# VectorE's difference of a weight unit placed one unit of eight tiles sooner in its order

## The chip, the cores and the metric

The kernel runs on one core of a Trainium2 chip. What counts is the device time of one execution in microseconds (us), the median of the runs; lower is better. A core has TensorE (PE, matrix products), VectorE (DVE), ScalarE (ACT), GpSimd (POOL) and SyncE (SP), which issues the loads. Each engine works through its own list of instructions in order, and waits at an instruction until the semaphores that it names have been raised.

## The reference

Two transformer blocks are computed in float32, one behind the other, for 256 tokens of width 2048, and the final norm:

- Block one: `mod = silu(c) @ w_ada`, six vectors that shift, scale and gate; `h = rmsnorm(x) * (1 + scale) + shift`; `p = h @ w_in`; a latent attention branch (norm, `w_uq`, `w_ukv`, rotary, causal softmax, `w_o_mla`); a gated delta rule branch (causal convolution of width 4 and silu on 24 groups of 128 channels, unit length rows, a triangular solve in chunks of 64, a running state, `w_o_gdn`); both gated by sigmoids and joined by `w_o`; then `silu(gate) * up` through `w_gate_up` and `w_down`.
- Block two: norm, `w_in_2`; a convolution of width 31 with layer norm and silu on half the channels and a neighbourhood attention with 16 heads on the other half; `w_out_2`; then `relu(h @ w_up_2) ** 2 @ w_down_2`, and the last norm.

## The kernel before, in words

All the weight matrices are cut into tiles of 128 x 128, put into one stream in the order in which PE uses them (6848 tiles), eight to a **unit** of 128 x 1024 floats, 512 KB. To keep accuracy in PE's float32r format, a unit is split in two: **HI**, the rounded weights (ACT, function hi, L566: a copy into float32r), and **LO**, what the rounding left (VectorE, function lo, L722: raw minus HI). The activations are split in the same way (split_hi on ACT, split_lo on VectorE, L758 and L760), and PE adds three products for a tile: in pairs of tiles L360, L361, L363 and L364 (called wide), else L366 to L368; for the last matrix L375 to L377, four tiles a step (tile_tokens). So PE can't begin a unit until its LO is there.

Buffers: RAW has 5 slots for loaded units, HI and LO have 3 each (NHL). HI and LO of unit v therefore overwrite those of unit v - 3, and wait until PE has ended that unit. RAW's slot is free when LO has run. Among the units of the stream stand others ("A" in the list of kinds), 512 KB each, of w_ada; these go through no PE, VectorE multiplies and sums each in one instruction (unit_dot, L710).

The order is written by one walk through the program (walk). Every engine goes through the same walk and puts down only its own instructions, so the place of a call in the walk is its place in the order of its engine. Products are made by blocks (16 tiles make one output of 128 columns, for a matrix with 2048 rows), and each block, when it ends, leaves a generator with its evacuation and what follows from it (later). Such generators, of attention and the delta rule too, stand in a list, and flush takes a step of each that is due: after tiles 1, 3, 5 and 7 of a unit, with at least LAG = 3 tiles from a step to the next, EVLAG = 4 before the first.

The feeding of units is also in that walk. At the end of unit u (i == 7) blocks sets unit_pe[u], calls feed(u + AHEAD), and then flush. feed(n) puts down the HI of all units up to n that have none (hi_part), then goes through the slots up to unit n in order (proc_next: lo for a unit of the stream, unit_dot for one of w_ada, and behind each the loads that it makes room for, load_next), and last it looks one unit on: if unit n + 1 has no HI yet, its load is put down and PE's end of the unit whose buffer it takes is known, its HI is put down as well. tile_tokens does the same from the function tokens. With AHEAD = 2 the end of unit u thus puts down LO(u+2) and, behind it, HI(u+3).

Names used below. g_less (L912) subtracts a product from MT or UU in the delta rule, and g_turn_mt (L467) transposes the outcome on PE; g_level (L908) and g_rows (L916) are neighbours of it on VectorE, g_copy (L671) on ACT, g_pair (L473) on PE. taps (L816) are three instructions of the convolution of width 4, followed by tanh (L581) and the next tap_first (L648) on ACT. rope_turn is L421. copy_sum (L570) and sum_halves (L726) evacuate a bank. SP's loads of the stream are L334.

Of the kernel before, what the change touches and what calls it, by code (L numbers as in the profile page):

```python
# [4 lines left out]

T = 256
NRAW, NEARLY, NHL = 5, 8, 3
LAG, EVLAG, AHEAD = 3, 4, 2
N_TILES = 6848
N_ADA = 192  # L10
LATE = [(2, 0), (2, 1), (3, 1), (4, 1), (3, 0), (4, 0), (5, 0), (5, 1)]
# [2556 lines left out]
```

## Time and profile before

| | before |
|---|---|
| median of 3 runs | 2768.66 us |
| lowest, highest | 2768.32, 2770.45 us |
| profiled execution, its own time | 2770.82 us |
| its span, first to last instruction | 2768.3 us |
| mean granted clock of PE in it | 0.992 of 2.4 GHz |
| PE busy | 2693.1 us, 97% |
| VectorE busy | 1932.0 us, 70% |
| ACT busy | 1318.2 us, 48% |
| POOL busy | 152.4 us, 6% |
| DMA, mean | 204 GB/s |

In the profile's rows L12 is line 12 of the kernel. A name such as LO<-RAW,HI gives what an instruction writes and reads. A matmul's end is modelled, since matmuls overlap in PE. "Idle before" is the engine's idle time in front of an instruction, with what ended it behind the arrow.

### The profile page before, as it was taken

To read this page: it belongs to the slowest core of one execution; us is meant where nothing else is said; L and a number is where in the kernel's file an instruction comes from. 1 tells how busy PE (TensorE), PEld (TensorE's weight loads), DVE (VectorE), ACT (ScalarE), POOL (GpSimd) and SP (SyncE) were. 2 spreads that over 40 slices of the span, in tenths; PEclk is the share of its full clock that TensorE was granted. 3 is DMA by queue.
4 is the path that set the end of the run, shared out by engine and by line. 5 is a ranking of instruction groups with operands and counts; after the bars stand their busy time and mean duration, and the time that the engine had idled before them with its cause. 6 is when DMAs were issued, how large, how long until landed. Compare 5 with 4: busy or idle time off the path is not lost.

```text
span 2768.3 us, 41005 instructions
## 1 busy us (share of the span) xinstructions
PE 2693.1 (97%) x16144; PEld 2386.3 (86%) x16144; DVE 1932.0 (70%) x2982; ACT 1318.2 (48%) x2063; POOL 152.4 (6%) x132
## 2 busy tenths in 40 slices
PE   8989999999999999999999999999999999999998
PEld 7778978888899888888888889998888888888887
DVE  6777778866886886566555678997667466575665
ACT  2175644433544544444444454467564444443443
POOL 0000000000002000000000170211100000000000
PEclk9999999999999999999999999999999999999999
DMA  9944358656796786555555555554545555655554
GB/s 387 409 142 157 106 183 276 225 191 198 266 317 215 256 297 208 191 189 190 187 188 191 187 177 165 184 166 138 170 154 177 195 190 191 194 186 197 189 191 145
DMA packets 158737, 565.17 MB, mean 204 GB/s; under 512 B 17617, under 2 KB 21841, under 8 KB 158417
## 3 DMA queue, kind: packets, MB, share of 16 engines
q1 hardware_dynamic: 158544, 562.56, 59.9%
q8 instruction: 127, 2.08, 0.3%
q14 instruction: 66, 0.53, 0.1%
HBM read 560.39 MB, written 2.10 MB: 203 GB/s over the span
## 4 chain that ended last, share of the span: by engine, by line
PE 86%; DVE 6%; ACT 3%; DMA 3%; issue 1%; DVEq 0%; POOL 0%; ACTq 0%; SPq 0%
PE BK L363 17%; PE BK L361 17%; PE BK L364 8%; PE BK L360 8%; PE BK L366 5%; PE BK L368 5%; PE BK L367 5%; PE BK L377 4%; PE BK L376 4%; PE BK L375 4%; PE BK L473 2%; DVE LO L722 2%; DMA EARLY<-wada_dram 1%; ACT HI L566 1%; PE BK L388 1%
## 5 line engine op out<-in xcount | busy, mean ns | idle before, releaser
L566 ACT ACTIVATE HI<-RAW 128x1024 fp32r<-128x1024 f32 x824 | 874.9, 1062 | 1182.0 <-PE BK L361 636.7
L722 DVE TENSOR_TENSOR LO<-RAW,HI 128x1024 fp32r<-128x1024 f32 x824 | 1012.3, 1229 | 384.8 <-ACT HI L566 383.6
L363 PE MATMUL BK<-H,HI 128*128 128x512 f32 x2160 | 871.6, 406 | 18.9 <-DVE LO L722 18.2
L361 PE MATMUL BK<-H,HI 128*128 128x512 f32 x2128 | 842.0, 397 | 0.0
L364 PE MATMUL BK<-H,LO 128*128 128x256 f32 x2160 | 602.6, 279 | 0.0
L360 PE MATMUL BK<-H,LO 128*128 128x256 f32 x2128 | 596.5, 280 | 0.2 <-DVE H L760 0.2
L360 PEld LDWEIGHTS BK<-H,LO 128*128 128x128 f32 x2128 | 402.0, 189 | 94.0 <-DVE H L760 0.6
L364 PEld LDWEIGHTS BK<-H,LO 128*128 128x128 f32 x2160 | 409.3, 189 | 84.9 <-issue 1.0
L363 PEld LDWEIGHTS BK<-H,HI 128*128 128x128 f32 x2160 | 412.5, 191 | 32.6 <-DVE LO L722 23.1
L361 PEld LDWEIGHTS BK<-H,HI 128*128 128x128 f32 x2128 | 401.7, 189 | 3.8
L366 PE MATMUL BK<-H,HI 128*128 128x256 f32 x1280 | 377.4, 295 | 7.1 <-DVE LO L722 6.4
L368 PE MATMUL BK<-H,LO 128*128 128x256 f32 x1280 | 363.9, 284 | 0.0
L367 PE MATMUL BK<-H,HI 128*128 128x256 f32 x1280 | 363.7, 284 | 0.0
L366 PEld LDWEIGHTS BK<-H,HI 128*128 128x128 f32 x1280 | 246.8, 193 | 10.7 <-DVE LO L722 8.2
L367 PEld LDWEIGHTS BK<-H,HI 128*128 128x128 f32 x1280 | 246.9, 193 | 1.4
L368 PEld LDWEIGHTS BK<-H,LO 128*128 128x128 f32 x1280 | 246.5, 193 | 0.0
L375 PE MATMUL BK<-HI,H 128*128 128x512 f32 x512 | 199.2, 389 | 0.0
L377 PE MATMUL BK<-HI,H 128*128 128x512 f32 x512 | 199.2, 389 | 0.0
L376 PE MATMUL BK<-LO,H 128*128 128x512 f32 x512 | 199.2, 389 | 0.0
L760 DVE TENSOR_TENSOR H<-TV,H 128x256 fp32r<-128x256 f32 x116 | 49.1, 425 | 171.5 <-ACT H L577 171.5
L376 PEld LDWEIGHTS BK<-LO,H 128*128 128x128 f32 x512 | 96.1, 188 | 20.1
L375 PEld LDWEIGHTS BK<-HI,H 128*128 128x128 f32 x512 | 96.1, 188 | 19.9
(266 smaller groups left out, 2555.0 us busy)
## 6 DMA issues: line engine op xcount, KB each, us to landing
RAW<-wst_dram SPq DMA_DIRECT2D x837, 512.0 KB, 3.4
RAW<-wada_dram SPq DMA_DIRECT2D x155, 512.0 KB, 4.6
EARLY<-wada_dram SPq DMA_DIRECT2D x37, 512.0 KB, 11.0
EARLY<-wst_dram SPq DMA_DIRECT2D x19, 512.0 KB, 12.2
X<-xT_dram SPq DMA_DIRECT2D x8, 512.0 KB, 7.0
B<-bias_dram SPq DMA_DIRECT2D x32, 128.0 KB, 3.4
out_dram<-B SPq DMA_DIRECT2D x8, 256.0 KB, 2.2
B<-gain_dram SPq DMA_DIRECT2D x1, 1024.0 KB, 4.8
```

The costliest lines, as they stand in the source:

```text
L360: e.matmul(bk[:, 256:512], ll, H[:, k, 0:256], start=False, stop=False, skip_group_check=True)
L361: e.matmul(bk[:, :], hh, H[:, k, :], start=False, stop=last, skip_group_check=True).then_inc(S["tile"], 1)
L363: e.matmul(bk[:, :], hh, H[:, k, :], start=first, stop=False, skip_group_check=True)
L364: e.matmul(bk[:, 256:512], ll, H[:, k, 0:256], start=False, stop=last, skip_group_check=True).then_inc(S["tile"], 1)
L366: e.matmul(bk[:, 0:256], hh, H[:, k, 0:256], start=first, stop=False, skip_group_check=True)
L367: e.matmul(bk[:, 0:256], hh, H[:, k, 256:512], start=False, stop=False, skip_group_check=True)
L368: e.matmul(bk[:, 0:256], ll, H[:, k, 0:256], start=False, stop=last, skip_group_check=True).then_inc(S["tile"], 1)
L375: e.matmul(bks[m][:, :], H[:, k, 128 * m:128 * m + 128], hh, start=first, stop=False, skip_group_check=True)
L376: e.matmul(bks[m][:, :], H[:, k, 128 * m:128 * m + 128], ll, start=False, stop=False, skip_group_check=True)
L377: r = e.matmul(bks[m][:, :], H[:, k, 256 + 128 * m:384 + 128 * m], hh, start=False, stop=last, skip_group_check=True)
L566: e.activation(HI[:, u % NHL, :], raw_at(slot), ACT.Copy).then_inc(S["hi"], 1)
L722: e.tensor_tensor(LO[:, u % NHL, :], raw_at(slot), HI[:, u % NHL, :].bitcast(f32), sub).then_inc(S["lo"], 1)
```

## The change

AHEAD goes from 2 to 3, so the end of unit u calls feed(u + 3). That puts down HI(u+3) and then the slots up to unit u+3, LO(u+3) the last of them. The look one unit on finds that PE's end of unit u + 1 isn't known yet and puts down nothing. HI(u+3) has the place that it had; LO(u+3), the unit_dots of the slots between LO(u+2) and LO(u+3), and the loads behind them, stand one unit sooner. The start (feed(w.tile // 8 + 2), after the direct products) is as it was.

```diff
--- before.py
+++ after.py
@@ -5,7 +5,7 @@
 
 T = 256
 NRAW, NEARLY, NHL = 5, 8, 3
-LAG, EVLAG, AHEAD = 3, 4, 2
+LAG, EVLAG, AHEAD = 3, 4, 3
 N_TILES = 6848
 N_ADA = 192
 LATE = [(2, 0), (2, 1), (3, 1), (4, 1), (3, 0), (4, 0), (5, 0), (5, 1)]
```

## Rows read from the trace of the kernel before

**Rows 1.** Page, part 1: busy us (share of the span) xinstructions.

```profile
PE 2693.1 (97%) x16144; PEld 2386.3 (86%) x16144; DVE 1932.0 (70%) x2982; ACT 1318.2 (48%) x2063; POOL 152.4 (6%) x132
```

**Rows 2.** Waits of PE, VectorE and SP: us in total, times, longest us.

```profile
PE BK L363 <- DVE LO L722: 18.2, 12, 5.3
...
PE BK L366 <- DVE LO L722: 6.4, 4, 4.3
...
DVE LO L722 <- ACT HI L566: 383.6, 357, 4.5
...
SPq L334 <- DVE LO L722: 1866.3, 765, 14.3
```

**Rows 3.** Timeline, quiet stage (start us, us, instruction [idle before]); busy us by engine 1040-1590.

```profile
1100.47 1.06 ACT L566 ACTIVATE HI<-RAW 128x1024 fp32r<-128x1024 f32 x1 [1.45 <-PE BK L361]
1101.57 1.23 DVE L722 TENSOR_TENSOR LO<-RAW,HI 128x1024 fp32r<-128x1024 f32 x1 [0.57 <-ACT HI L566]
...
1103.26 1.06 ACT L566 ACTIVATE HI<-RAW 128x1024 fp32r<-128x1024 f32 x1 [1.72 <-PE BK L364]
...
1040.00:1590.00 550.00, 549.76 (x3154) 479.30 (x3153) 330.54 (x440) 259.90 (x371) 9.57 (x8) 1.00 0.57 191
```

**Rows 4.** Timeline of PE: two waits for LO and one for ACT.

```profile
166.46 0.80 PE L363 MATMUL BK<-H,HI 128*128 128x512 f32 x1 [5.33 <-DVE LO L722]
...
321.05 0.33 PE L499 MATMUL BK<-CN,B 128*128 128x128 f32 x1 [1.49 <-ACT B L644]
...
509.00 0.50 PE L363 MATMUL BK<-H,HI 128*128 128x512 f32 x1 [2.07 <-DVE LO L722]
```

**Rows 5.** Stretches: length, PE, PEld, DVE, ACT, POOL busy, granted clock, DMA share, GB/s.

```profile
165.79:172.62 6.83, 6.16 (x20) 5.30 (x21) 4.51 (x11) 6.72 (x9) 0.00 (x0) 0.50 0.29 93
...
510.54:513.95 3.41, 3.41 (x14) 3.03 (x13) 3.34 (x8) 3.38 (x5) 0.00 (x0) 0.50 0.97 381
...
321.05:324.46 3.41, 3.41 (x30) 3.41 (x31) 1.68 (x5) 2.80 (x8) 0.00 (x0) 1.00 0.49 157
```

**Rows 6.** Timeline of one level of the delta rule; all instructions of L912.

```profile
628.37 1.06 ACT L566 ACTIVATE HI<-RAW 128x1024 fp32r<-128x1024 f32 x1 [2.47 <-PE BK L368]
...
628.00 0.68 DVE L912 TENSOR_TENSOR X<-X,BK 128x512 f32<-128x512 f32 x1
...
629.52 0.60 PE L467 MATMUL BK<-CN,X 128*128 128x128 f32 x4
...
L912 DVE TENSOR_TENSOR X<-X,BK x20: 677/687/690, 283.7 to 662.2; 128x512 f32<-128x512 f32 x20
L912 DVE TENSOR_TENSOR B<-B,BK x8: 679/686/693, 359.9 to 684.1; 64x512 f32<-64x512 f32 x8
```

**Rows 7.** Instructions of L816, 176 to 222; timeline of ACT behind one group.

```profile
L816 DVE SCALAR_TENSOR_TENSOR TV<-B,CO,TV x30: 475/482/485, 179.5 to 219.5; 128x255 f32<-128x255 f32 x10, 128x254 f32<-128x254 f32 x10, 128x253 f32<-128x253 f32 x10
...
193.62 1.52 DVE L816 SCALAR_TENSOR_TENSOR TV<-B,CO,TV 128x255 f32<-128x255 f32 x3
...
195.18 0.42 ACT L581 ACTIVATE B<-TV 128x256 f32<-128x256 f32 x1 [1.56 <-DVE TV L816]
...
196.16 1.05 ACT L566 ACTIVATE HI<-RAW 128x1024 fp32r<-128x1024 f32 x1
```

**Rows 8.** Timeline of ACT, VectorE and PE in the mixed stage.

```profile
294.68 1.06 ACT L566 ACTIVATE HI<-RAW 128x1024 fp32r<-128x1024 f32 x1 [1.00 <-PE BK L368]
...
293.97 1.28 DVE L916 TENSOR_TENSOR X<-BK,B 128x512 f32<-128x512 f32 x2
...
296.18 0.59 PE L421 MATMUL BK<-B,CN 128*128 128x256 f32 x2
```

**Rows 9.** Timeline at a seam of the feed-forward part.

```profile
1077.44 0.42 DVE L726 TENSOR_TENSOR TV<-BK,TE 128x256 f32<-128x256 f32 x1
...
1077.98 1.06 ACT L566 ACTIVATE HI<-RAW 128x1024 fp32r<-128x1024 f32 x1 [1.46 <-PE BK L361]
...
1079.86 0.50 PE L363 MATMUL BK<-H,HI 128*128 128x512 f32 x1
```

## The prediction

> **What bounds the kernel now.** I read the page first, for the busy time by engine [rows 1]: TensorE (PE) is busy for 97% of 2768.3 us and VectorE (DVE) for 70%. So the time is PE's, and only PE's gaps can be gained or added. The view of waits by engine comes next [rows 2]. PE waited 18.2 + 6.4 = 24.6 us for VectorE's LO, in 16 waits; VectorE itself sat idle for 383.6 us, in 357 gaps, in front of LO until ACT's HI was there. The second number matters more: VectorE works in order and stops at an instruction whose signal is missing.
>
> The timeline of a quiet stage shows the clockwork [rows 3]. HI of unit v overwrites the buffer of unit v-3, so it starts when PE ends that unit: one HI every 2.79 us, 1.06 us long. LO follows 0.04 us behind HI, 1.23 us long, although its place in the order is a unit later: VectorE has run ahead of PE to that place. PE is busy for 549.76 of the 550 us there. So LO can't come sooner in the quiet stages: HI isn't moved, and LO needs it.
>
> **What the change does.** feed(u + 3) at the end of unit u puts LO(u+3) where LO(u+2) stood. HI(u+3) was already put there by the look-ahead at the end of feed, so ACT's and PE's orders stay. With LO move the dots (L710) of the slots before it, and SP's loads, which follow each LO or dot. Nothing is added or removed; no load is larger.
>
> SP costs nothing: it waited 1866.3 us for LO in all [rows 2], so its queue has room, and a load can only be issued sooner. If a load did become late, HI would be, but it has the rest of two units, over 3 us.
>
> **Gain.** LO is no longer behind other VectorE work, so the 16 waits [rows 2] can go, 24.6 us. At six of them, the 5.33 us at 166.46 and the 2.07 us at 509.00 among them [rows 4], PE's granted clock then falls to 0.50, which is 1.2 GHz: for 6.83 us in two of the six cases (as at 165.79) and for 3.4 us in four (as at 510.54) [rows 5], 27.3 us, of which half, 13.7 us, is lost work. The ends are 0 and 38.3 us. I take 31: two of the waits lie in the stage of rows 7, where LO is late again.
>
> **Cost.** VectorE now stands at LO(u+3) until PE has ended unit u and HI is through, and only then does what stands behind: the steps put down at that unit's end. Those with a reader on PE four tiles later are late. One is seen whole [rows 6]. HI starts at 628.37, ends at 629.43; LO would then run from 629.5 to 630.7, and g_less (L912, now at 628.00, 0.68 us) end at 631.3 or 631.4. PE's transposes of it (L467) started at 629.52. So PE waits **1.9 us**. Before, LO's place there was filled by one whose HI had been ready for a unit.
>
> A. This repeats in the levels of the delta rule. L912 runs 20 + 8 times [rows 6]; going through the timeline I count 18 with a PE reader so close: 18 x 1.9 = **34 us**.
>
> B. In the mixed stage from 205 to 340 (convolution, latent attention and delta rule at once) the same happens to g_rows (L916 at 293.97, twice, 1.28 us): HI starts at 294.68, so the LO would end at 297.0 and L916 at 298.3 at the earliest, and PE's L421, which waits for its signal, ran at 296.18 [rows 8]: 2.1 us. I count ten such; taken at 1.8 us each, between A's size and this one's less what a few tenths of spare take off, they make 18 us.
>
> C. From 176 to 222 there is a loop through both engines: HI 1.05, LO 1.22, three taps 1.52, then from tanh at 195.18 to the next HI at 196.16 another 0.98 us [rows 7], 4.8 us with the hand-overs. Before, the taps stood behind the LO of the unit before, so a turn of the loop took in two units; now it is one, against PE's 2.8 us. x30 are ten units with taps [rows 7], 2.0 us each; LO's lead of some 3 us and the six units without taps give back 6: 14 us.
>
> D. Three seams of the feed-forward part (1080, 1331, 1571): L726 at 1077.44 begins the split whose end the tile at 1079.86 needs [rows 9]. Behind HI (from 1077.98) and LO it would begin at 1080.3, 2.9 us later. ACT's part of the split stands behind that HI today, which I estimate to give back 0.6 us: 2.2 us each, 6.7 in all.
>
> E. Three more at 2046 to 2058, where normed rows go VectorE, ACT, PE, by A's size: 6.
>
> F. Single ones (770 to 805, 1672, 1779, 1892): about 8, which no row fixes; ends 0 and 15.
>
> B to F are 53 us. Some fall into one unit, where one wait covers the other, so I take two thirds: **35 us**. Ends: 15 and 53. For A: half, 17, if VectorE often reaches the place late anyway, and 34.
>
> G. The clock again. A wait of 1.49 us at 321.05 cost no clock, and one of 2.07 did [rows 4, 5]. The new ones, near 1.9, lie between, nearer to the second. The 18 of A and some 12 of the others, by 1.7 us (half of 3.4), would be 51; the other end is 0. Since their sizes spread over the gap between the two rows, I take half, **25 us**.
>
> Sum: 34 + 35 + 25 - 31 = +63 us. The profiled execution took 2770.8 us (its span is 2768.3) and lies 2.2 us over the median of the runs, 2768.66. So 2770.8 + 63 - 2.2 = **2832 us**, 2.3% slower.
>
> The Trainium skill, Perfetto Trace Analysis, section Optimization Strategy, speaks for the change: find the gaps on the most contended engine, see what signal ends them, and make that dependency start sooner. The trace has such gaps, 24.6 us for LO; by that rule alone the sum would be the gain, -38 us, and the time that of R1 or a little less. The same page of the Trainium skill, section Sequencer Loop, has an engine's instruction wait in its queue until its semaphore is ready; the trace agrees, with 383.6 us of VectorE standing in front of LO.
>
> **Rivals.** R1, **faster**: VectorE has 30% of its time free and absorbs the standing; only the gain is left. It decides at the readers: if L912's result were due later than 631.4, A would be nothing. For it: 16 waits and six clock falls are real. Against: 629.52 is a reader's start on an engine that never idles. It gives 2768.7 - 31 = 2737 us. Chance 0.10.
>
> R2, **no difference**: LO already runs right behind HI in fact, so the new place changes nothing where it matters, or gain and cost cancel: A at half and B to F at their low end, 32, less 31. 2769 us. It also stands for the change not doing what it says. For it: rows 3. Chance 0.06.
>
> R3, **the loop of C in more stages**, with VectorE to ACT to HI in each unit, as in latent attention's tail and the convolution, and the clock falling at all new waits: 34 + 53 + 51 - 31 = 107, to 2876 us. For it: ACT feeds on VectorE in many stages, and VectorE is busy for 70% of the span [rows 1] even with nothing to stand for. Against: the loop bites only where it is longer than PE's unit in most units, and only x30 of L816, of all the taps, stand so close [rows 7]. Chance 0.20.
>
> **How the numbers follow.** The forecast has 0.64. Its own range takes A whole, B to F from 15 to 53 and G from 10 to 40, about 2797 to 2865. The range of 8 in 10 is 2778 to 2885: it leaves out R1, R2 and a tail of R3. A measurement of this kernel can tell about 0.2%, 5.5 us, from no change. Slower by more: 0.64 + 0.20 = 0.84; within it 0.06; faster 0.10.
>
> **What would show it.** Right: in the profile after, PE's waits for LO are near 0, but L467 and L473 wait for VectorE's X (L912), about 1.9 us each and over ten times; VectorE's idle time in front of LO grows beyond 383.6 us; the granted clock falls more often than before between 400 and 700; the stretches 1100 to 1300 and 2145 to 2700 take as long as before. Wrong: L467 with no wait for VectorE (A fails and R1 holds), or waits in every unit from 176 to 222 and at 1600 (R3). If A's waits are there with the clock at 1.00 throughout, G was too large, and the time is near 2807.

## The result, and the profile after

| | before | after |
|---|---|---|
| median | 2769.16 us (4 runs) | 2947.10 us (4 runs) |
| lowest, highest | 2768.32, 2770.45 us | 2940.32, 2953.70 us |
| span of the profiled execution | 2768.3 us | 2949.8 us |
| mean granted clock | 0.992 | 0.976 |

The changed kernel is slower by the factor 1.0643, interval 1.0617 to 1.0668: +178 us where +63 was forecast, outside the range of 2778 to 2885. The sign was right, the size was not.

The page of the changed kernel, part 1, answers to [rows 1], and its part 5 has LO:

```profile
PE 2748.5 (93%) x16144; PEld 2419.5 (82%) x16144; DVE 1930.4 (65%) x2982; ACT 1316.4 (45%) x2063; POOL 126.8 (4%) x132
...
L722 DVE TENSOR_TENSOR LO<-RAW,HI 128x1024 fp32r<-128x1024 f32 x824 | 1012.9, 1229 | 920.6 <-ACT HI L566 858.9
```

VectorE does the same work as before, 1930.4 us in 2982 instructions. What grew is its standing in front of LO: 858.9 us for HI, against 383.6 [rows 2]. PE's side has two parts. It is idle for 2949.8 - 2748.5 = 201.3 us, before 75.2: +126.1. And the same 16144 matmuls take 55.4 us longer, 2748.5 against 2693.1, at a lower clock. The two make the 181.5 us of the span. Most of the second part is the clock: the mean granted clock lacks 0.8% of 2768.3 us before, 22 us, and 2.4% of 2949.8 us after, 71 us. The difference of 49 us is an estimate from the two rows of the table.

The waits of the changed kernel, of PE, VectorE and SP's queue (us in total, times, longest):

```profile
PE BK L363 <- DVE LO L722: 28.4, 18, 5.6
PE BK L499 <- ACT B L644: 28.1, 18, 6.0
PE BK L467 <- DVE X L912: 17.2, 11, 2.8
...
PE BK L485 <- DVE B L912: 5.1, 3, 1.8
...
PE BK L473 <- DVE X L912: 3.3, 2, 1.7
...
DVE LO L722 <- ACT HI L566: 858.9, 642, 7.6
DVE LO L722 <- PE BK L361: 49.4, 34, 2.1
...
SPq L334 <- DVE LO L722: 2103.8, 765, 12.7
```

Two things are to be seen. The waits for LO, which the change should have ended, are there as before: 28.4 us for L363 alone, against 24.6 in all [rows 2]. They have moved: 19.0 us of them, in nine waits, lie in units 35 to 53 (8.5 us in two before), and none lies in units 103 to 184 (3.8 us in three before). And two families are new: readers of L912, 25.6 us in 16 waits, and L499 behind ACT's L644, 28.1 us in 18, of which 19.3 us in 12 lie in units 530 to 560. Over all rows of this view, PE's waits for VectorE went from 32.4 us in 24 to 116.5 in 78, and those for ACT from 26.3 us in 46 to 68.4 in 69.

Next, where it happened. I count time from the first matmul of one unit of the stream to that of another. The same stretches of work, before, as windows (length, PE, PEld, DVE, ACT, POOL busy, granted clock, DMA share, GB/s): units 35 to 53 (taps), 53 to 83 (mixed), 103 to 184 (delta rule), 530 to 560 (wide convolution and neighbourhood attention):

```profile
158.20:224.60 66.40, 57.51 (x299) 49.03 (x298) 54.43 (x106) 44.66 (x79) 0.00 (x0) 0.92 0.43 142
224.60:368.60 144.00, 138.37 (x967) 126.92 (x966) 102.50 (x201) 85.84 (x199) 0.00 (x0) 1.00 0.38 125
462.30:774.90 312.60, 303.91 (x2042) 274.22 (x2040) 235.38 (x365) 134.69 (x207) 0.00 (x0) 0.99 0.69 229
1779.40:1898.70 119.30, 118.64 (x930) 116.58 (x929) 109.64 (x221) 71.26 (x150) 20.00 (x22) 0.99 0.48 161
```

And after, the same units, with the quiet ones from 608 to 855 last:

```profile
158.30:246.80 88.50, 66.14 (x299) 54.02 (x298) 56.04 (x107) 45.17 (x79) 0.00 (x0) 0.85 0.31 105
246.80:425.70 178.90, 151.78 (x968) 136.62 (x967) 105.64 (x206) 86.87 (x199) 0.00 (x0) 0.93 0.32 106
...
527.60:882.90 355.30, 318.37 (x2042) 284.04 (x2040) 235.64 (x366) 135.96 (x207) 0.00 (x0) 0.96 0.61 200
1921.70:2066.90 145.20, 123.59 (x931) 118.55 (x929) 107.46 (x219) 68.65 (x147) 17.15 (x21) 0.97 0.39 127
2250.90:2934.80 683.90, 681.46 (x3447) 577.88 (x3446) 414.80 (x530) 307.24 (x395) 0.00 (x0) 1.00 0.56 186
```

The losses are 22.1, 34.9, 42.7 and 25.9 us, 125.6 in the four. In each the length less PE's busy time has grown (8.9 to 22.4, 5.6 to 27.1, 8.7 to 36.9, 0.7 to 21.6), and so has the busy time itself. The rest are units 83 to 103 (+8.2), 184 to 264 (+9.3), 264 to 480 (+12.6, of which the three seams 11.2), 480 to 530 (+12.4) and 560 to 608 (+13.3). The quiet units take 683.9 us in both.

One level of the delta rule, unit 141, as a timeline; it is the work of [rows 6]:

```profile
715.58 1.06 ACT L566 ACTIVATE HI<-RAW 128x1024 fp32r<-128x1024 f32 x1 [2.47 <-PE BK L368]
...
716.68 1.22 DVE L722 TENSOR_TENSOR LO<-RAW,HI 128x1024 fp32r<-128x1024 f32 x1
717.82 0.68 DVE L912 TENSOR_TENSOR X<-X,BK 128x512 f32<-128x512 f32 x1
718.56 0.66 PE L467 MATMUL BK<-CN,X 128*128 128x128 f32 x4 [1.66 <-DVE X L912]
```

Before, L912 stood ahead of HI's end; now it stands behind HI and LO, and PE waits 1.66 us, where 1.9 were forecast.

In the taps (ACT, VectorE and PE; one turn of the loop):

```profile
196.98 1.04 ACT L566 ACTIVATE HI<-RAW 128x1024 fp32r<-128x1024 f32 x1
...
198.05 1.23 DVE L722 TENSOR_TENSOR LO<-RAW,HI 128x1024 fp32r<-128x1024 f32 x1 [1.23 <-ACT HI L566]
199.53 1.51 DVE L816 SCALAR_TENSOR_TENSOR TV<-B,CO,TV 128x255 f32<-128x255 f32 x3
...
201.08 0.42 ACT L581 ACTIVATE B<-TV 128x256 f32<-128x256 f32 x1 [3.06 <-DVE TV L816]
202.06 1.04 ACT L566 ACTIVATE HI<-RAW 128x1024 fp32r<-128x1024 f32 x1
```

And the turn that I had not worked out, in units 530 to 560:

```profile
1992.99 1.05 ACT L566 ACTIVATE HI<-RAW 128x1024 fp32r<-128x1024 f32 x1
...
1994.07 1.23 DVE L722 TENSOR_TENSOR LO<-RAW,HI 128x1024 fp32r<-128x1024 f32 x1 [1.82 <-ACT HI L566]
1995.21 1.67 DVE L934 SCALAR_TENSOR_TENSOR B<-B,CO 128x256 f32<-128x256 f32 x4
...
1996.80 0.16 DVE L876 RECIPROCAL SC<-SC 128x1 f32<-128x1 f32 x1
...
1996.99 0.51 ACT L644 ACTIVATE B<-B,SC 128x256 f32<-128x256 f32 x1 [2.68 <-DVE SC L876]
...
1998.69 1.06 ACT L566 ACTIVATE HI<-RAW 128x1024 fp32r<-128x1024 f32 x1
```

The "..." stand for rows left out. Both read in the same way. HI lets LO go, LO the steps behind it on VectorE, those ACT's step, and the next HI stands behind that step on ACT. From HI to HI it is 5.1 us in the first and 5.7 in the second. Before, a unit of the second stage took PE 119.3 / 30 = 3.98 us; after, 145.2 / 30 = 4.84. The turn does not close in every unit: ACT's L644 waits for VectorE's L876 21 times in these 30 units, 61.0 us, where it was 13 times and 15.5 us before. In the taps the turn reaches PE through LO, as the nine waits above.

### The profile page after: what moved, and what is told of

Read it like the earlier page. It is cut to its first block, busy times and chain, and to the rows that moved or that the text cites. A ratio compares the mean times of both kernels' runs of the same rounds, so it can differ in the third digit from the quotient of the medians.

```text
span 2949.8 us, 41058 instructions
## 1 busy us (share of the span) xinstructions
PE 2748.5 (93%) x16144; PEld 2419.5 (82%) x16144; DVE 1930.4 (65%) x2982; ACT 1316.4 (45%) x2063; POOL 126.8 (4%) x132
## 4 chain that ended last, share of the span: by engine, by line
PE 76%; DVE 11%; ACT 7%; issue 3%; DMA 2%; POOL 0%; DVEq 0%; SPq 0%; ACTq 0%; POOLq 0%
PE BK L363 15%; PE BK L361 15%; PE BK L364 7%; PE BK L360 7%; DVE LO L722 4%; PE BK L375 4%; ACT HI L566 4%; PE BK L376 4%; PE BK L377 4%; PE BK L366 4%; PE BK L368 4%; PE BK L367 4%; DMA EARLY<-wada_dram 2%; DVE B L934 1%; PE BK L473 1%
## 5 line engine op out<-in xcount | busy, mean ns | idle before, releaser
L722 DVE TENSOR_TENSOR LO<-RAW,HI 128x1024 fp32r<-128x1024 f32 x824 | 1012.9, 1229 | 920.6 <-ACT HI L566 858.9
L363 PE MATMUL BK<-H,HI 128*128 128x512 f32 x2160 | 878.9, 409 | 33.5 <-DVE LO L722 28.4
L360 PE MATMUL BK<-H,LO 128*128 128x256 f32 x2128 | 599.5, 282 | 2.4 <-DVE H L760 2.4
L360 PEld LDWEIGHTS BK<-H,LO 128*128 128x128 f32 x2128 | 405.5, 191 | 97.6 <-DVE H L760 2.8
L364 PEld LDWEIGHTS BK<-H,LO 128*128 128x128 f32 x2160 | 413.1, 191 | 85.9 <-issue 1.0
L363 PEld LDWEIGHTS BK<-H,HI 128*128 128x128 f32 x2160 | 416.4, 193 | 50.8 <-DVE LO L722 36.9
L361 PEld LDWEIGHTS BK<-H,HI 128*128 128x128 f32 x2128 | 404.8, 190 | 3.7
L366 PE MATMUL BK<-H,HI 128*128 128x256 f32 x1280 | 384.2, 300 | 16.9 <-DVE TV L768 6.3
L367 PE MATMUL BK<-H,HI 128*128 128x256 f32 x1280 | 369.0, 288 | 0.0
L366 PEld LDWEIGHTS BK<-H,HI 128*128 128x128 f32 x1280 | 253.3, 198 | 21.9 <-issue 5.4
L367 PEld LDWEIGHTS BK<-H,HI 128*128 128x128 f32 x1280 | 252.9, 198 | 1.6
L368 PEld LDWEIGHTS BK<-H,LO 128*128 128x128 f32 x1280 | 252.3, 197 | 0.0
L375 PEld LDWEIGHTS BK<-HI,H 128*128 128x128 f32 x512 | 96.1, 188 | 21.4 <-DVE LO L722 1.6
L377 PEld LDWEIGHTS BK<-HI,H 128*128 128x128 f32 x512 | 96.1, 188 | 20.0
## 6 DMA issues: line engine op xcount, KB each, us to landing
EARLY<-wst_dram SPq DMA_DIRECT2D x19, 512.0 KB, 12.6
```

What stands on the lines that cost most here:

```text
L360: e.matmul(bk[:, 256:512], ll, H[:, k, 0:256], start=False, stop=False, skip_group_check=True)
L361: e.matmul(bk[:, :], hh, H[:, k, :], start=False, stop=last, skip_group_check=True).then_inc(S["tile"], 1)
L363: e.matmul(bk[:, :], hh, H[:, k, :], start=first, stop=False, skip_group_check=True)
L364: e.matmul(bk[:, 256:512], ll, H[:, k, 0:256], start=False, stop=last, skip_group_check=True).then_inc(S["tile"], 1)
L366: e.matmul(bk[:, 0:256], hh, H[:, k, 0:256], start=first, stop=False, skip_group_check=True)
L367: e.matmul(bk[:, 0:256], hh, H[:, k, 256:512], start=False, stop=False, skip_group_check=True)
```

## The experiments

Theory: all of it is VectorE's standing in its own order, twice over: steps behind the wait are late for PE (delta rule, seams), and where an ACT step depends on them a loop through HI forms (taps, mixed stage, units 530 to 560). Rivals: the sooner dots and loads do harm; the wait is enough without LO; the loss is one that builds up over the stages, and not local ones.

### The parts of the change, each by itself

The kernel before stood at 2768.66 us here. First the dots alone, placed sooner; LO stays:

```diff
+            def feed_dots(u):
+                feed(u)
+                while st["proc"] < len(kinds) and kinds[st["proc"]] == "A":
+                    proc_next()
...
-                            feed(u + AHEAD)
+                            feed_dots(u + AHEAD)
```

> Edit: only the w_ada dots that stand between two units of the stream, and the loads behind them, are put down one unit sooner; LO stays where it was. Theory of the standing (VectorE stops at the new LO until PE has ended a unit and HI is through, and what stands behind it is late): this part costs nothing, 2760 to 2775 us. Rival of the dots (the sooner dots and loads crowd VectorE or the DMA queue): 2850 us or more.

Measured: 2759.28 us, 0.9963 (0.9950 to 0.9976). The part is no cost but a gain of 9 us, 6.2 of it in units 103 to 184 (306.4 us against 312.6). PE's waits for LO are 22.4 us in 12 instead of 24.6 in 16, and ACT's waits for a load in front of HI fell from 83.1 to 25.4 us; which of them makes the gain was not tested. The dots of w_ada and the loads behind them, by themselves, are cleared as a cause.

Then the wait alone. VectorE stands where it stands in the changed kernel until HI(u+3) is there, but no work is moved:

```diff
                             feed(u + AHEAD)
+                            stand(u + 3)
                             w.flush()
```

> Edit: LO, dots and loads stay where they were; VectorE only waits for the signal of HI(u+3) at the end of unit u, the place where the change puts LO(u+3). Theory of the standing: most of the loss comes with the wait alone, 2830 to 2900 us, less than the changed kernel's 2947 because LO's own 1.2 us isn't in front of the steps. Rival of the order (LO's 1.2 us ahead of the chains' steps costs, not the wait): 2785 us at most. Rival of the dots: 2769 us.

Measured: 2837.07 us, 1.0244 (1.0228 to 1.0259): +68, less than half of the loss: inside the theory's range, but not the "most" that it spoke of, and far above the rival of the order. Units 103 to 184 take 336.1 us, half of the way from 312.6 to 355.3. PE's waits in that stretch, and the window:

```profile
PE BK L366 <- DVE LO L725: 5.8, 2, 5.4
PE BK L363 <- DVE LO L725: 3.4, 4, 2.7
PE BK L467 <- DVE X L915: 3.0, 6, 0.6
PE BK L485 <- DVE B L915: 2.2, 4, 0.7
...
482.70:818.80 336.10, 311.10 (x2042) 276.99 (x2040) 236.94 (x368) 137.35 (x208) 0.00 (x0) 0.98 0.64 215
```

(Lines are three further on here: L915 is L912.) The readers of L912 wait here too, but no more than 0.7 us, where the full change, with LO's 1.2 us on top, has up to 1.8. And LO, still a unit later in the order, is itself late, 9.2 us in six waits: a loss that the full change doesn't have in this stage. Over the whole run it is 40.2 us in 27 waits, against 24.6 in 16. PE's busy time there grows by 7.2 us, half of the full change's 14.5. Units 530 to 560 take 123.3 us. There LO is still done ahead, in the time that HI takes, and I read the turn as shorter by its 1.23 us: 5.7 - 1.2 = 4.5 us. That is argued from the rows only.

Then LO one unit sooner, but behind the steps of the unit's end:

```diff
                             feed(u + AHEAD)
                             w.flush()
+                            feed(u + AHEAD + 1)
```

> Edit: LO(u+3) is put down at the end of unit u as in the change, but behind the steps that flush puts down there; HI keeps its place. Theory of the standing: steps of the unit's end are free again, so L467's waits for L912 are gone, but the steps of tiles 1, 3 and 5 still stand behind LO: 2800 to 2880 us. Rival of the dots: as the changed kernel, about 2945 us.

Measured: 2825.72 us, 1.0197 (1.0180 to 1.0214), +57. The windows of the delta rule and of units 530 to 560:

```profile
480.30:790.60 310.30, 302.21 (x2041) 272.83 (x2040) 234.63 (x365) 134.49 (x208) 0.00 (x0) 1.00 0.70 232
...
1807.20:1952.70 145.50, 124.04 (x929) 118.63 (x928) 106.78 (x219) 68.48 (x147) 17.10 (x21) 0.97 0.38 127
```

This run separates the two mechanisms. The 42.7 us of the delta rule are gone (310.3 against 355.3), since L912 comes out of flush and stands ahead of LO again: PE's waits for L912 are 0.8 us in two. Step A is shown. The 26 us of units 530 to 560 are all there, since the attention's steps there are put down when blocks yields, behind both feeds, all the same: L499 waits 28.1 us for L644, as in the changed kernel. The taps lost 6.9 us and the mixed stage 12.4, a third each.

Last, LO put down in the middle of the next unit, `feed(u + AHEAD)` once more at i == 3, ahead of flush:

> Edit: LO(u+2) is put down after tile 3 of unit u, half a unit sooner than in the kernel before and half a unit later than in the changed one; HI(u+2) was put down at the end of unit u-1. Theory of the standing: HI is through 1.1 us after the unit's end, tile 3 is 1.4 us behind it, so VectorE hardly stands and PE's waits for LO go: 2740 to 2775 us. Rival of the order: half of the loss, about 2860 us.

Measured: 2786.24 us, 1.0060 (1.0045 to 1.0075), +17.6. The delta rule (308.3) and units 530 to 560 (117.8) have nothing left. But the whole is outside the theory's 2740 to 2775 us: PE's waits for LO didn't go (22.5 us in 15), and what remains is spread over six stages with 2 to 5 us each. It was not followed up.

### One stage alone

The full change between units 103 and 184, the old order elsewhere:

```diff
-                            feed(u + AHEAD)
+                            feed(u + (3 if 103 <= u < 184 else AHEAD))
```

> Edit: LO one unit sooner at the ends of units 103 to 183 alone, the stage of the delta rule; everywhere else as in the kernel before. Theory of the standing: the loss is local, the 42.8 us that this stage lost in the changed kernel: 2805 to 2820 us. If the loss is built up over stages (a lead that is spent early and missed later), it is under 25 us here.

Measured: 2811.06 us, 1.0152 (1.0137 to 1.0168), +42.4. The stage takes 354.0 us, +41.4; of the rest no stage differs by more than 3 us. So this stage's loss is its own, and next to nothing is handed on. The other stages were not run alone.

```profile
PE BK L467 <- DVE X L912: 11.1, 8, 1.7
...
461.50:815.50 354.00, 316.61 (x2042) 282.08 (x2040) 235.66 (x365) 135.76 (x207) 0.00 (x0) 0.97 0.61 202
```

### HI with a buffer more

If HI is ready a unit sooner, there should be nothing to stand for. HI gets a fourth buffer, and to make room for it RAW has four slots and not five; the pair differs in AHEAD alone (the lines that index HI by NHI are left out here):

```diff
-NRAW, NEARLY, NHL = 5, 8, 3
+NRAW, NEARLY, NHL, NHI = 4, 8, 3, 4
```

> Edit: four HI buffers and four RAW slots in place of three and five, LO's place as in the kernel before (AHEAD 2). HI(u+4) can then be put down at the end of unit u. It is the partner for the next run; RAW's missing slot may cost something: 2765 to 2830 us by every theory.

Measured: 2778.76 us, 1.0042 (1.0025 to 1.0059).

> Edit: the same buffers with LO one unit sooner (AHEAD 3). HI(u+3) is through a unit before LO(u+3) wants it, so VectorE waits for PE's unit end alone, and a loop from VectorE over ACT to HI and LO takes in two units. Theory of standing and loop: 0 to 45 us over hi4_two. Rival of the order (LO ahead of the chains' steps is what costs): 100 us or more over hi4_two, as the 178 us of the change.

Measured: 2850.34 us, 1.0299 (1.0283 to 1.0314), 71.6 over its partner, between what theory (0 to 45) and rival (100) had given. The waits of VectorE in it:

```profile
DVE LO L722 <- PE BK L361: 373.4, 368, 6.3
DVE LO L722 <- PE BK L377: 162.7, 125, 1.8
DVE LO L722 <- PE BK L368: 84.3, 55, 3.6
DVE LO L722 <- PE BK L364: 50.0, 41, 2.7
...
DVE LO L722 <- ACT HI L566: 36.9, 36, 6.0
```

The wait for HI is nearly gone, but LO's own buffer comes free when PE ends unit u, so VectorE stands for PE: 670.4 us in the four rows, against 472.4 us in the partner, where LO already waits for PE and only 55.8 us for HI. That VectorE would wait for PE's unit end was expected; that this costs 71.6 us was not. By stages: the loops' loss is gone (35 to 53: -1.7 us against the partner; 530 to 560: +2.7), the mixed stage loses 8.2 us instead of 34.9, while the delta rule still loses 23.5 and units 83 to 103 lose 15.1. The last is also where w_ada's slots lie between, and RAW has one slot less in this pair, so I leave those 15 us open.

### The two loops cut

In the taps, ACT's tanh is put down one step later than the taps on VectorE, so that it need not stand ahead of the next HI:

```diff
                     v = do("taps", "ev_v", t, B1[:, j, :], COLS["conv_w"][0] + 4 * j, a, n=3)
+                    yield
                     s1 = do("tanh", "ev_a", B1[:, j, :], t, 1.0, v)
```

> Edit: in the convolution's chain the tanh on ACT is a step of its own, put down later than the taps that it reads; LO as before. Partner for the next run: 2765 to 2790 us.

Measured: 2757.56 us, 0.9965 (0.9952 to 0.9978).

> Edit: the same with AHEAD 3. Between HI and the next HI, ACT no longer waits for taps that stand behind LO, so the loop HI, LO, taps, tanh, HI is open. Theory of the loop: units 35 to 53, 22 us longer by the change, are now at most 10 us longer than in tanh_later_two, and the whole at most 165 us over it. Theory of standing with late readers alone: units 35 to 53 stay 20 us or more longer, the whole about 178 us.

Measured: 2910.58 us, 1.0518 (1.0502 to 1.0533), 153 over its partner, where the uncut pair differs by 178. Units 35 to 53 of the pair:

```profile
156.50:215.90 59.40, 52.94 (x294) 45.90 (x293) 49.24 (x92) 38.72 (x65) 0.00 (x0) 0.94 0.48 158
```

```profile
157.50:225.00 67.50, 57.87 (x294) 48.69 (x293) 47.15 (x89) 39.05 (x65) 0.00 (x0) 0.90 0.41 135
```

The loss there is 8.1 us instead of 22.1, in the mixed stage 23.6 instead of 34.9. Of the other stages the delta rule loses 35.3 us in this pair instead of 42.7, and units 83 to 103 16.4 instead of 8.2. So the loop was at work in the taps. For the 23.6 us left in the mixed stage two causes stand in the rows of the changed kernel, and no run takes them apart: readers on PE, as step B has it, and further loops over ACT. Of the reader that B named, L421 behind L916, there is one wait; ACT's L635 waits for VectorE's L872 for 18.1 us where it was 5.7 before. In units 53 to 83 (the rows are of two views, PE's waits and ACT's):

```profile
PE BK L421 <- DVE X L916: 2.6, 1, 2.6
...
ACT B L635 <- DVE SC L872: 18.1, 10, 3.1
```

That the mixed stage loses only 8.2 us in the pair with four HI buffers speaks for the loops.

In the neighbourhood attention, ACT's exponential and scaling are moved a unit behind the VectorE instructions that they wait for (for this attention alone; the edit also lets the attention's steps run one longer, which is left out here):

```diff
+                def t1(i):
+                    mst[i].append(do("soft_max", "at_v", mst[i][1], 3 * (i % 32), mst[i][2]))
+
+                def t2(i):
+                    pi, p, _, v = mst[i]
+                    a = do("soft_exp", "at_a", p, 3 * (i % 32), v)
+                    mst[i] = [pi, p, do("soft_share", "at_v", 3 * (i % 32), a)]
+
+                def t3(i):
+                    pi, p, v = mst[i]
+                    mst[i] = [pi, p, do("soft_scale", "at_a", p, 3 * (i % 32), v)]
-                return [s0, s1, s2, s2b, s3]
+                return [s0, t1, t2, t3, s2b, s3] if split else [s0, s1, s2, s2b, s3]
```

> AHEAD = 2 as before; in the neighbourhood attention ACT's exponential and scaling are put down one unit behind the VectorE instruction that they wait for. Partner of the next run. Theory of the loop: nothing is bound by a loop at AHEAD = 2, so units 530 to 560 take 116 to 120 us (119.3 before) and the whole 2765 to 2773 us. Rival: the attention's softer order already gives something, below 2763.

Measured: 2773.51 us, 1.0015 (1.0006 to 1.0025); units 530 to 560 take 121.8 us. Both are a little above what was expected, 2773 and 120.

> The full change (AHEAD = 3) with the same edit: ACT's exponential and scaling are behind the next HI, so ACT doesn't wait for VectorE in front of HI. Theory of the loop HI, LO, L934 and L876, ACT, HI: units 530 to 560 fall from 145.2 to under 127 us and the whole is 18 to 30 us under the changed kernel, 2917 to 2929, with the other stages as they were. Rival (the 26 us come from VectorE's load behind LO or from the clock, no loop): units 530 to 560 stay at 138 or more, and the whole at 2940 or more.

Measured: 2921.99 us, 1.0548 (1.0530 to 1.0566), 25 under the changed kernel. Its waits and its window of units 530 to 560:

```profile
PE BK L499 <- ACT B L644: 2.0, 2, 1.5
...
1913.40:2040.60 127.20, 119.80 (x919) 116.09 (x919) 112.94 (x227) 68.83 (x147) 17.82 (x23) 0.97 0.46 155
```

The whole is where the theory had it; the stage is at 127.2 us, where under 127 was expected, and the rival's 138 is ruled out. The stage loses 5.4 us against its partner instead of 25.9, and the 28.1 us of L499 behind L644 are 2.0. Of the 25 us, 18.0 are this stage's and 7.8 are units 480 to 530, where L499 waited once for L644, 6.0 us. The second loop is shown.

### What is left to gain

Both harmless parts together, the dots sooner and tanh later, at AHEAD = 2:

> Edit: the w_ada dots and their loads one unit sooner, and the tanh of the convolution's chain a step of its own; LO as in the kernel before. The two gained 9 and 11 us in different stages: 2746 to 2756 us if they add up, 2757 if they don't.

Measured: 2753.05 us, 0.9943 (0.9931 to 0.9956). Then tanh as a step of its own in the first of the convolution's two chains alone (heads 0 to 3 of the delta rule), and LO in the middle of a unit from unit 608 on:

> Edit: as dots_tanh, but tanh a step of its own only in the first of the two chains, where it gained, and LO after tile 3 in units from 608 on, where VectorE has little else: 2741 to 2752 us.

Measured: 2750.54 us, 0.9935 (0.9923 to 0.9947). Both beat the kernel before; they differ from each other by less than can be told. Only 4.5 of the 18 us are what the change was after: PE's waits for LO in the last are 20.1 us, against 24.6 [rows 2]. PE's busy time is 2682.1 us, 11.0 less than before.

```profile
PE BK L363 <- DVE LO L722: 13.6, 7, 6.5
...
PE BK L366 <- DVE LO L722: 6.5, 4, 4.3
```

## Why the prediction was wrong in size

The sum came to +63 us and the change cost 178, 115 more. Three steps of the sum make most of that: the gain of 31 us didn't come; the loop through VectorE and ACT in units 530 to 560, 25.9 us, had no term; and the clock was taken at some 11 us net where PE's busy time grew by 55.4. (The first and the last overlap in the gain's 13.7 us of clock.) Of the signs that the forecast named for itself the first failed, since PE's waits for LO are 29.2 us and not near 0; the others came: L467 and L473 wait for L912 13 times, 1.6 us each, and the quiet stages take as long as before.

**The bound and the sign: right.** PE's gaps set the time, VectorE stood at LO as it was said (383.6 to 858.9 us), and the quiet stages didn't change. SP cost nothing. R1 and R2 fell: VectorE's free 30% absorbed none of the standing where a reader on PE was a few tiles away. No load became late: ACT waits 18.9 us for loads in front of HI, 83.1 before.

**Gain, -31: wrong, it didn't come.** LO's 16 waits were to go because LO stands behind nothing any more. They are 20 (L363's 18 and two of L366), 29.2 us. LO's place is sooner in the list, but in the taps' loop VectorE reaches it later: nine of the waits, 19.0 us, are there, where the forecast left two. Outside the taps they fell from 16.1 us in 14 to 10.2 in 11; in the delta rule they are gone, elsewhere new ones came.

**A, 34: right in mechanism, somewhat large.** The stage of the delta rule grew by 42.7 us, 28.2 of it idle. I counted 18 readers at 1.9 us; there are 16 at 1.6, 25.6 us in the three rows above, 19.5 of it in this stage. The rest of its idle time is behind other steps of VectorE, such as L925 (3.7 us) and L884 (2.8 us). lo_behind_steps takes it away and three_103_184 brings it alone.

**B, 18 (12 after the two thirds): too small.** The mixed stage has 21.5 us more of idle time; a third of its loss is the taps' loop, by the tanh pair (34.9 to 23.6). B's own mechanism was counted ten times; L916 with a reader on PE shows as two waits there, 4.1 us.

**C, 14 (9 after the two thirds): right in place and turn.** 4.8 us was forecast for the turn and 5.1 measured, and the idle time grew by 13.5.

**The loop between 530 and 560: the step that failed first.** R3 had it for other stages, the latent attention's tail and the convolution, and held against it that of the taps only thirty stand close enough. I had looked for the loop at L816 and not at any other VectorE instruction with an ACT step behind it, such as L876 and L644. It costs 25.9 us, 20.9 of it idle, and the sum held nothing for it but single waits of F.

**D, 6.7: right.** PE waits at the three seams for VectorE's split (L760), 4.2 us for L363 in two waits and 2.4 for L360 in one, 6.6 us in all. The seams are longer by 11.2 us, 3.7 each, because a stretch of 3.4 us at a granted clock of 0.50 or 0.51 follows at each of them (from 1199.1, 1455.1 and 1697.5), of which half, 1.7 us, is lost. That is G's part.

**E, 6: right; F, 8: too small.** E's readers are in the trace: L399 waits for ACT's L589, which stands behind VectorE's rows, 2.6, 2.6 and 1.2 us at 2224.0, 2231.4 and 2238.8 (6.6 us in all in units 560 to 608, 1.0 before). Units 184 to 264, 480 to 530 and 560 to 608 together lost 35 us, 27 of it idle, so F's single ones are more or longer than counted. No run took them apart.

**The two thirds on B to F: wrong way.** I let waits cover one another and took 35 us for 53. Without the delta rule and units 530 to 560, PE's idle time grew by 77.0 us (126.1 - 28.2 - 20.9), more than even the undiscounted 53. stand_alone's +68 and the +57 of lo_behind_steps can't be set against the whole 178, since each has the wait in it and neither is a clean part. They do show that wait and LO work together: in the delta rule standing alone makes L912's readers 0.7 us late at most and the full change 1.8, and units 530 to 560 lose 4.0 us by the wait alone and 25.9 with LO behind it.

**G, 25, with -13.7 in the gain: the other step that failed.** Net, the clock was to cost some 11 us; PE's busy time grew by 55.4, of which the mean granted clock explains some 49. Of the two ends, 0 and 51, the second was nearer. Half was taken because the new waits lay between one of 1.49 us that cost no clock and one of 2.07 that did, but waits of A's size do cost it. In the changed kernel, the reader of L912 at 545.81 and what follows it:

```profile
545.81 0.93 PE L485 MATMUL BK<-B,X 64*128 64x128 f32 x6 [1.67 <-DVE B L912]
...
547.20:554.03 6.83, 6.83 (x28) 6.30 (x27) 0.97 (x2) 0.94 (x1) 0.00 (x0) 0.50 0.59 205
```

The loops' waits, which the sum for 530 to 560 did not have, add to it. No run changes the clock without the waits, so its share rests on the busy time of the same matmuls and the granted clock beside it.

The Trainium skill, Perfetto Trace Analysis, section Optimization Strategy, would have the dependency that the most contended engine waits for start sooner. dots_alone agrees in part: PE's waits for LO fell by 2.2 us and the time by 9. For LO, which has its own wait in front, the runs do not.

Together R3 had most of the mechanisms and, at 2876, still too little: 71 us less than measured, of which the gain that did not come is 31 and the stage from 530 to 560 another 26.

**Open:** what makes up F's share of the 35 us, and the 8.2 us of units 83 to 103, for which the sum held nothing; how the 23.6 us left in the mixed stage divide; units 83 to 103 in the hi4 pair; what is left of lo_tile_3's 17.6 us.

## What to carry to other kernels

Before an instruction is moved up on an in-order engine, ask what it waits for at the new place: everything behind it inherits that wait, and an engine with 30% of free time gave none of it here to the reader that is four tiles away. Look for each turn that closes through two queues (here HI, LO, any VectorE step, the ACT step that reads it, the next HI), and compare its length to the unit of the bounding engine, for every stage and not for the one where it was found. Move the parts that have little to wait for at the new place (here the dots, -9 us) and leave the rest, or put the dependent ACT step later: that took 14 us back in the taps and 20 in the neighbourhood attention.

## What the hardware showed that was not expected

PE's loss is only two thirds idle time. The same 16144 matmuls took 2748.5 us instead of 2693.1, with the mean granted clock at 0.976 instead of 0.992; in the taps it was 0.85 instead of 0.92 and the busy time 66.1 us instead of 57.5. PE's busy time thus grew by nearly half as much as its idle time (55.4 on 126.1). Long waits are not needed for it: in the delta rule, where L912's readers wait 1.8 us at most and no wait of PE is above 2.6, the clock is 0.96 and the busy time 318.4 us against 303.9, and three waits of 1.6 to 1.8 us (L485 behind L912, at 545.8, 562.2 and 785.6) are each followed by 6.8 us at a granted clock of 0.50 (from 547.2, 564.3 and 786.1). The forecast's row of a wait of 1.49 us that cost no clock [rows 4, 5] was one case and did not stand for these.
